# A two-block transformer kernel: the norm boundaries of block 2 multiply x by the root of the mean square, and a token's scale is applied when a product leaves PSUM

## The chip, the cores and the metric

The kernel runs on one core of a Trainium2 chip. The metric is the device time of one execution in microseconds (us), of which three runs are shown below; less is better. One further execution was profiled, and its trace is what the rows below come from.

## The reference

Everything is float32, for 256 tokens of width 1024. Block 1 (a recurrent mixer, a windowed attention and an FFN) is the same in both kernels except for its very last step. Block 2 takes the 256 tokens with 16 meta tokens ahead of them (272 columns) through two layers, and each layer crosses three norm boundaries:

```python
def rmsnorm(x, gain):
    xf = x.astype(jnp.float32)
    y = xf * lax.rsqrt(jnp.mean(xf * xf, axis=-1, keepdims=True) + RMS_EPS)
    return (y * gain.astype(jnp.float32)).astype(x.dtype)

def swiglu(h, w_gu, w_down):
    gate, up = jnp.split(h @ w_gu, 2, axis=-1)
    return (jax.nn.silu(gate) * up) @ w_down

for l in range(DEPTH_2):
    h = h + 0.5 * rmsnorm(swiglu(rmsnorm(h, g_pre_ffn1[l]), w_ffn1_gu[l], w_ffn1_down[l]), g_post_ffn1[l])
    mix = token_mixer(rmsnorm(h, g_pre_mix[l]), key_valid, ...)
    h = h + rmsnorm(mix, g_post_mix[l])
    h = h + 0.5 * rmsnorm(swiglu(rmsnorm(h, g_pre_ffn2[l]), w_ffn2_gu[l], w_ffn2_down[l]), g_post_ffn2[l])
```

The token mixer projects h by one wide matrix, runs softmax attention over 8 heads ("fox") and gated linear attention over 4 heads ("gla"), merges both under two sigmoid gates and projects again.

## The kernel before

Activations lie with features on the 128 partitions: x is 8 tiles of 128 x 272. A weight matrix streams through in panels. SyncE loads a panel into `land` (two slots, by the panel's parity), ScalarE rounds it to fp32r into `w_hi` (`split_hi`, L615), VectorE subtracts to get `w_lo` (`split_lo`, L622), and TensorE does three matmuls for each 128x128 tile: w_hi by h_hi, w_hi by h_lo, w_lo by h_hi (`tile_mm`, L640 to L642). While TensorE works on panel p, ScalarE and VectorE split panel p+1's successor of the same parity, always one panel ahead of need. `section` runs such a stage, two panels for each pass of a hardware loop, the last ones written out.

An FFN is 22 gate/up panels of 16 tiles (48 matmuls; `pe_project`, `act_gate_up`, `dve_gate_up`) and 8 down panels of 22 tiles (`pe_down`, `act_products`, `dve_products`). In a gate/up panel ScalarE takes the sigmoid of the gate from PSUM (L931), VectorE multiplies twice from PSUM (L945, L947), and both split the result into a_hi (L934) and a_lo (L953). PSUM has room for two gate/up panels.

At a boundary the last panel's squares close the sum `ssum`; `pe_stat` spreads their mean over the partitions with one matmul by `mean_ones` (L795, in full float32, two passes); ScalarE takes the root (`act_root`, L805), VectorE the reciprocal (L811), then for each of 8 tiles f = f * gain * rstd (L914) and x = x + f (L917). `act_pre_sums` squares x (L820), `pe_pre` sums the squares (L870), and a second root and a second reciprocal follow before `dve_pre_apply` normalises (L849), ScalarE rounds h_hi (L834), and VectorE subtracts h_lo (L860). Only then does the next section's first matmul start. Block 2 has six such boundaries, called b=1 to b=6 here: b=1 and b=4 lead from a down section into a gate/up section, b=2 and b=5 from a down section into the mixer's projection (whose first three panels have 8 tiles), b=3 and b=6 from the mixer's output projection (two output tiles to a panel) into a gate/up section.

In the mixer, 14 projection panels are cut in halves ("chunks", 24 matmuls each, `pe_chunk`), and TensorE places the small matmuls of fox and gla between them in an order written out by hand in `pe_mixer`. ScalarE empties most chunks from PSUM, taking the sigmoid at once where the chunk is a merge gate (L1781), VectorE the rest (L1798); a chunk's split is by `act_chunk_split` and `dve_chunk_split`, in the program order of those engines. GpSimd zeroes some tiles and copies fox's keys (L1936).

Of the kernel before, what the change touches and what calls it, by code (L numbers as in the profile page):

```python
# [922 lines left out]


# [1746 lines left out]
```

## Time and profile before

| | us |
|---|---|
| three runs | 2294.39, 2298.12, 2304.79 (median 2298.12) |
| the profiled execution | 2301.5 |
| its span in the trace | 2299.7 |
| TensorE matmul busy | 2038.5 (89%) |
| VectorE busy | 1357.4 (59%) |
| ScalarE busy | 953.1 (41%) |
| GpSimd busy | 115.8 (5%) |
| mean granted TensorE clock | 0.909 of full |

A matmul's record runs from its start to its modelled end, so records overlap, and the pace of a stretch is the distance between starts. Idle time in brackets names the instruction that ended it. A window of the rows below runs from the last matmul of a section to the end of the next one's first panel; its last numbers are the granted clock, the busy share of DMA and GB/s. The chain of waits follows the work that ended last back to the start.

### The profile page before, as it was taken

What the parts mean: (1) busy time and instruction counts of PE and PEld (TensorE: products, weight loads), DVE (VectorE), ACT (ScalarE), POOL (GpSimd) and SP (SyncE); (2) the same over time, 40 slices, a digit from 0 to 9 for tenths busy, and PEclk for the clock granted to TensorE, in tenths of its full rate; (3) what the DMA queues carried; (4) which work ended last, traced back from release to release, by engine and by line L of the source; (5) the groups of instructions that cost most, each with busy time, mean ns of one, the idle gap of its engine ahead of it and who ended that gap; (6) DMA issues with size and microseconds to landing.
All of it is one profiled execution on the core that took longest, in us unless ns stands there. A gap on an engine that the chain in (4) does not pass through costs nothing.

```text
span 2299.7 us, 38236 instructions
## 1 busy us (share of the span) xinstructions
PE 2038.5 (89%) x14904; PEld 1949.6 (85%) x14904; DVE 1357.4 (59%) x2065; ACT 953.1 (41%) x1382; POOL 115.8 (5%) x138
## 2 busy tenths in 40 slices
PE   8899548888789988998999879997999799798997
PEld 7899438886679988997888869997999788787997
DVE  5977545444676556555655575655655565566664
ACT  2333243332355434543443345533553354345542
POOL 0510001000000000000300000000000200000000
PEclk7899677777799999999999899998999999798998
DMA  7575000000335534552422244552455233253552
GB/s 316 201 259 218 0 24 1 0 0 18 113 128 182 198 131 146 172 198 97 147 74 94 83 156 146 166 193 99 164 181 185 97 101 106 76 166 126 183 199 94
DMA packets 43384, 301.21 MB, mean 131 GB/s; under 512 B 4689, under 2 KB 6881, under 8 KB 11025
## 3 DMA queue, kind: packets, MB, share of 16 engines
q1 hardware_dynamic: 42688, 296.90, 37.1%
q0 software_dynamic: 592, 2.87, 0.4%
q8 instruction: 74, 1.21, 0.2%
q14 instruction: 30, 0.24, 0.0%
HBM read 298.70 MB, written 1.05 MB: 130 GB/s over the span
## 4 chain that ended last, share of the span: by engine, by line
PE 78%; DVE 11%; ACT 4%; DVEq 3%; issue 2%; DMA 1%; POOL 0%; ACTq 0%; POOLq 0%; SPq 0%
PE acc L640 20%; PE acc L642 20%; PE acc L641 20%; DVE w_lo L622 3%; ACT w_hi L615 2%; PE acc L2012 1%; PE mb L870 1%; DVE rstd L811 1%; PE mb L709 1%; PE mb L1458 1%; PE acc L1458 1%; PE mb L1984 1%; PE acc L1455 1%; DVE f L914 1%; DVEq L1020 1%
## 5 line engine op out<-in xcount | busy, mean ns | idle before, releaser
L640 PE MATMUL acc<-h_hi,w_hi 128*128 128x272 f32 (+1 forms) x3040 | 893.5, 294 | 66.2 <-DVE w_lo L622 30.4
L642 PE MATMUL acc<-h_hi,w_lo 128*128 128x272 f32 (+1 forms) x3040 | 884.0, 291 | 0.0
L641 PE MATMUL acc<-h_lo,w_hi 128*128 128x272 f32 (+1 forms) x3040 | 882.9, 290 | 0.0
L622 DVE TENSOR_TENSOR w_lo<-land,w_hi 128x2048 fp32r<-128x2048 f32 (+2 forms) x257 | 590.7, 2300 | 230.0 <-ACT w_hi L615 229.3
L640 PEld LDWEIGHTS acc<-h_hi,w_hi 128*128 128x128 f32 x3040 | 590.9, 194 | 74.7 <-issue 38.5
L642 PEld LDWEIGHTS acc<-h_hi,w_lo 128*128 128x128 f32 x3040 | 590.7, 194 | 0.0
L641 PEld LDWEIGHTS acc<-h_lo,w_hi 128*128 128x128 f32 x3040 | 590.4, 194 | 0.2
L615 ACT ACTIVATE w_hi<-land 128x2048 fp32r<-128x2048 f32 (+2 forms) x257 | 490.8, 1911 | 224.7 <-PE acc L642 158.6
L640 PE MATMUL acc<-a_hi,w_hi 128*128 128x272 f32 (+1 forms) x880 | 251.0, 285 | 0.8 <-DVE w_lo L622 0.7
L642 PE MATMUL acc<-a_hi,w_lo 128*128 128x272 f32 (+1 forms) x880 | 250.5, 285 | 0.0
L641 PE MATMUL acc<-a_lo,w_hi 128*128 128x272 f32 (+1 forms) x880 | 250.0, 284 | 0.0
L931 ACT ACTIVATE sig<-acc 128x272 f32<-128x272 f32 (+1 forms) x110 | 43.3, 394 | 305.3 <-PE acc L642 305.3
L640 PEld LDWEIGHTS acc<-a_hi,w_hi 128*128 128x128 f32 x880 | 165.4, 188 | 1.8 <-DVE w_lo L622 1.8
L641 PEld LDWEIGHTS acc<-a_lo,w_hi 128*128 128x128 f32 x880 | 165.8, 188 | 0.0
L642 PEld LDWEIGHTS acc<-a_hi,w_lo 128*128 128x128 f32 x880 | 165.3, 188 | 0.0
L881 ACT ACTIVATE sq_post<-acc 128x256 f32<-128x256 f32 (+1 forms) x64 | 23.8, 391 | 263.8 <-PE acc L642 263.8
L945 DVE TENSOR_TENSOR t_ff<-sig,acc 128x272 f32<-128x272 f32 (+1 forms) x110 | 47.5, 432 | 131.6 <-ACT sig L931 131.6
L898 DVE COPY f<-acc 128x256 f32<-128x256 f32 (+3 forms) x64 | 27.7, 433 | 148.7 <-ACT sq_post L881 147.8
L870 PE MATMUL mb<-sq,mean_ones 128*128 128x272 f32 (+1 forms) x128 | 52.3, 570 | 41.3 <-ACT sq L820 40.8
L870 PEld LDWEIGHTS mb<-sq,mean_ones 128*128 128x128 f32 x128 | 28.4, 266 | 64.8 <-ACT sq L820 55.5
L640 PE MATMUL acc<-y_hi,w_hi 128*128 128x256 f32 (+1 forms) x192 | 57.4, 299 | 16.1 <-DVEq L506 13.6
L931 ACT ACT_TABLE_LOAD x50 | 64.2, 1283 | 0.9
(473 smaller groups left out, 2445.3 us busy)
## 6 DMA issues: line engine op xcount, KB each, us to landing
land<-in_w_gu SPq DMA_DIRECT2D x110, 1024.0 KB, 4.9
land<-in_w_in SPq DMA_DIRECT2D x65, 1024.0 KB, 4.9
land<-in_w_down SPq DMA_DIRECT2D x40, 1408.0 KB, 6.1
ada_first<-in_w_ada SPq DMA_DIRECT2D x24, 1024.0 KB, 8.4
land<-in_w_ab SPq DMA_DIRECT2D x24, 512.0 KB, 3.6
land<-in_w_out SPq DMA_DIRECT2D x12, 1024.0 KB, 4.9
land<-in_w_in_single SPq DMA_DIRECT2D x6, 512.0 KB, 3.5
const<-in_const POOLq DMA_DIRECT2D x1, 1134.0 KB, 5.3
```

The source lines that it names most:

```text
L615: k.nc.scalar.activation(k.w_hi[:, p.par, 0:size * P], k.land[:, p.par, 0:size * P], ACT.Copy).then_inc(k.hi_ready, 1)
L622: k.nc.vector.tensor_tensor(k.w_lo[:, p.par, 0:size * P], k.land[:, p.par, 0:size * P], k.w_hi[:, p.par, 0:size * P].bitcast(F32), ALU.sub ...
L640: mm(out, k.w_hi[:, par, c], hi, start=start, stop=False)
L641: mm(out, k.w_hi[:, par, c], lo, start=False, stop=False)
L642: return mm(out, k.w_lo[:, par, c], hi, start=False, stop=stop)
L709: last = k.nc.tensor.matmul(k.mb[:, 2, n * 2 + o:n * 2 + o + 1], w[:, o, t], k.csil_mean[:, t:t + 1], start=t == 0, stop=t == KT - 1)
L870: k.nc.tensor.matmul(k.mb[:, 3, 0:W.stop - W.start], k.mean_ones[:, :], k.sq[:, t % 2, W], start=t == 0, stop=t == KT - 1).then_inc(k.sq_u ...
L881: k.nc.scalar.activation(k.sq_post[:, 2 * p.par + o, W], k.acc[:, 2 * p.par + o, 0:n], ACT.Square).then_inc(k.sq_post_ready, 1)
L898: v.tensor_copy(f, k.acc[:, 2 * p.par + o, 0:n])
L931: k.nc.scalar.activation(k.sig[:, p.par, W], k.acc[:, 2 * p.par, 0:n], ACT.Sigmoid).then_inc(k.sig_ready, 1)
L945: v.tensor_tensor(k.t_ff[:, p.par, W], k.sig[:, p.par, W], k.acc[:, 2 * p.par, 0:n], ALU.mult)
L1458: last = mm(bank[:, 1, c * P + lo:c * P + hi], m["x_bd"][:, c, :], m["xr"][:, c, lo:hi], start=True, stop=True)
```

## The change

In words, with the root r = sqrt(mean f^2 + eps) of the branch's output f: the kernel before builds x' = x + gain * f / r and then normalises x'. The changed kernel builds z = x * r + gain * f, which is r times x', and does not normalise it: h_hi and h_lo are split from z * gain, the projection runs on that, and each column (token) of the product is multiplied by 1 / sqrt(mean z^2 + eps * r^2) as it leaves PSUM.

- At the end of a section (`act_products_z`, `dve_products_z`) the gain is applied as f leaves PSUM, ScalarE loads the table of the root early (`warm`), and the second panel of the next section is split into a third weight buffer, `w3_hi` and `w3_lo`. `pe_stat_z` adds the last panel's squares by matmul.
- `act_z`, `dve_z` make z, h_hi and h_lo. `pe_project_z` runs the next section's first panel tile by tile as h_lo comes, with nine float32 matmuls of z's squares (eight tiles and the eps term) among its own, and the second panel from the third buffer.
- `dve_scale` takes the reciprocal of the scale (into `ssum`'s place). Gate/up panels (`act_gate_up_z`, `dve_gate_up_z`) multiply gate and up by it first (`t_ff`, `g_ff`), then take the sigmoid from SBUF, and do a_lo a panel later. In the mixer every chunk leaves PSUM by a VectorE multiply, and ScalarE takes the gates' sigmoids from SBUF afterwards.
- After two gate/up panels (in the mixer, after the three small panels) `dve_undo` takes 1/r, and GpSimd restores x' = z / r with one instruction over all 8 tiles (`pool_z`). In the mixer GpSimd's zeroing comes after that.
- In the mixer, TensorE does one more chunk ahead of gla's output matmuls (and the rest of gla moves by one chunk), on VectorE and ScalarE likewise.

```diff
+def pe_project_z(k, pe, b, start, count, tiles, W, loop=0):
...
+    p = Panel.of(start, loop)
+    panel_begin(k, pe, p)
+    for t in range(KT):
+        pe.wait_ge(k.hl_ready, (b + 1) * KT + (t + 1))
+        for o in range(tiles):
+            last = tile_mm(k, k.acc[:, 2 * p.par + o, 0:n], p.par, o * KT + t, k.h_hi[:, t, W], k.h_lo[:, t, W],
+                           t == 0, t == KT - 1)
+        if t == KT - 1:
+            last.then_inc(k.panel_done, 1)
+        if t > 0:
+            square_sum(t - 1)
+    square_sum(KT - 1)
+    square_sum(KT)
```

```diff
+    for o in range(tiles):
+        pe.wait_ge(k.sq_post_ready, b * KT + KT - tiles + o + 1)
+        r = k.nc.tensor.matmul(stat, k.mean_ones[:, :], k.sq_post[:, 2 * last.par + o, W], start=False,
+                               stop=o == tiles - 1)
+    r.then_inc(k.stat_done, 1)
...
+    def one(t, p, ahead_size):
+        act.wait_ge(k.panel_done, p.count(3))
+        for o in range(tiles):
+            k.nc.scalar.activation(k.sq_post[:, 2 * p.par + o, W], k.acc[:, 2 * p.par + o, 0:n],
+                                   ACT.Square).then_inc(k.sq_post_ready, 1)
+        if ahead_size == "same":
+            split_hi(k, act, p.ahead2(), size)
+        elif ahead_size == "next":
+            split_hi(k, act, p.ahead2(), nxt)
+            split_hi_third(k, act, Panel.of(start + count + 1, loop), nxt)
+            k.nc.scalar.activation(k.warm[:, b:b + 1], k.eps[:, 0:1], ACT.Sqrt)
+    section(act, start, count, one, loop, ("next", None), unrolled=True)
...
+    def square(t):
+        act.wait_ge(k.sq_used, first + t + 1)
+        a(k.sq[:, (first + t) % 2, W], k.x[:, t, W], ACT.Square).then_inc(k.sq_ready, 1)
+    act.wait_ge(k.stat_done, b + 1)
+    act_root(k, post)
+    for t in range(KT):
+        act.wait_ge(k.z_ready, (b - 1) * KT + (t + 1))
+        a(k.h_hi[:, t, W], k.x[:, t, W], ACT.Copy, scale=gain(t)).then_inc(k.hh_ready, 1)
+        if t > 0:
+            square(t - 1)
+    square(KT - 1)
+    act.wait_ge(k.sq_used, first + KT + 1)
+    a(k.sq[:, (first + KT) % 2, W], k.root[:, W], ACT.Square, scale=float(np.sqrt(8 * EPS))).then_inc(k.sq_ready, 1)
+    act.wait_ge(k.sq_used, first + KT + 3)
+    a(k.scale[:, W], k.mb[:, 2, 0:W.stop - W.start], ACT.Sqrt).then_inc(k.scale_root, 1)
+
+
...
+    v = k.nc.vector
...
+    for t in own:
+        v.tensor_tensor(k.x[:, t, W], k.x[:, t, W], k.root[:, W], ALU.mult)
+    dve.drain()
...
+        v.tensor_tensor(k.x[:, t, W], k.x[:, t, W], k.f[:, t, W], ALU.add).then_inc(k.z_ready, 1)
...
+    def rest(t):
+        dve.wait_ge(k.hh_ready, (b + 1) * KT + (t + 1))
+        v.scalar_tensor_tensor(k.h_lo[:, t, W], k.x[:, t, W], gain(t), k.h_hi[:, t, W].bitcast(F32), ALU.mult,
+                               ALU.subtract).then_inc(k.hl_ready, 1)
+    for t in range(KT):
+        z(t)
+        if t > 1:
+            rest(t - 2)
+    rest(KT - 2)
+    rest(KT - 1)
...
+def dve_undo(k, dve, b, W):
+
+    k.nc.vector.reciprocal(k.rstd[:, W], k.root[:, W]).then_inc(k.r_ready, 1)
...
+    g.tensor_tensor(k.x[:, :, W], k.x[:, :, W], over(k.rstd[:, W], KT), ALU.mult)
+    pool.drain().then_inc(k.x_done, 1)
...
+    def one(t, p, ahead_size):
+        ahead(split_hi, k, act, p, ahead_size, GU_K)
+        act.wait_ge(k.t1_ready, z * FT + (t + 1))
+        k.nc.scalar.activation(k.sig[:, p.par, W], k.t_ff[:, p.par, W], ACT.Sigmoid).then_inc(k.sig_ready, 1)
+        act.wait_ge(k.a_ready, z * FT + (t + 1))
+        k.nc.scalar.activation(k.a_hi[:, bass.ds(t, 1), W].rearrange("p a n -> p (a n)"), k.a_ff[:, p.par, W],
+                               ACT.Copy).then_inc(k.ah_ready, 1)
...
+    def one(t, p, ahead_size, behind=True):
+        dve.wait_ge(k.panel_done, p.count(3))
+        v.tensor_tensor(k.t_ff[:, p.par, W], k.acc[:, 2 * p.par, 0:n], c, ALU.mult).then_inc(k.t1_ready, 1)
+        v.tensor_tensor(k.g_ff[:, p.par, W], k.acc[:, 2 * p.par + 1, 0:n], c, ALU.mult).then_inc(k.acc_free, 1)
+        if behind:
+            rest(t - 1, 1 - p.par)
+        ahead(split_lo, k, dve, p, ahead_size, GU_K)
+        dve.drain()
+        dve.wait_ge(k.sig_ready, i * FT + (t + 1))
+        v.tensor_tensor(k.t_ff[:, p.par, W], k.sig[:, p.par, W], k.t_ff[:, p.par, W], ALU.mult)
+        dve.drain()
+        v.tensor_tensor(k.a_ff[:, p.par, W], k.t_ff[:, p.par, W], k.g_ff[:, p.par, W],
+                        ALU.mult).then_inc(k.a_ready, 1)
+    one(0, Panel.of(start, loop), "same", False)
+    one(1, Panel.of(start + 1, loop), "same")
+    dve_undo(k, dve, b, W)
+    section(dve, start + 2, GU - 2, lambda t, p, s: one(t + 2, p, s), loop, nxt)
+    dve.drain()
+    rest(GU - 1, Panel.of(start + GU - 1, loop).par)
```

```diff
-        k.nc.vector.tensor_copy(dst(i), k.acc[:, 2 * p.par:2 * p.par + tiles, 0:n]).then_inc(k.acc_free, 1)
-        if signal is not None:
-            k.nc.vector.drain().then_inc(signal, 1)
+        k.nc.vector.tensor_tensor(dst(i), k.acc[:, 2 * p.par:2 * p.par + tiles, 0:n], over(k.scale[:, 0:n], tiles),
+                                  ALU.mult).then_inc(k.acc_free, 1)
         ahead(split_lo, k, dve, p, ahead_size, size)
     section(dve, start, count, one, loop, nxt)
...
+def act_chunk_gate(k, act, l, c):
+
+    r, o = divmod(c, 2)
+    if o == 0:
+        act.wait_ge(k.chunk_free, l * MIXED + r + 1)
+    else:
+        act.wait_ge(k.acc_free, mixed_panel(l, r).count(3))
+    return k.nc.scalar.activation(chunk_tile(k, l, c), chunk_tile(k, l, c), ACT.Sigmoid)
...
@@ -1917,7 +2198,8 @@
         pool.wait_ge(k.dec_mm, l)
     pool.dma_start(k.wal[:, :], flat(d["wal"], l)).then_inc(k.dec_in, 16)
     steps, first = fox_steps(l)
-    pool.wait_ge(k.hl_ready, (l * 3 + 4) * KT)
+    pool_z(k, pool, l * 3 + 2, W2)
+    pool.wait_ge(k.panel_done, Panel.of(M_LAYER + L_SINGLE + 1, l * (L_PANELS // 2)).count(3))
     g.memset(k.sel8[:, :, :].bitcast(F32), 0.0)
...
+    pe_chunk(k, pe, l, at + 6)
 
     for s in STREAMS:
...
             last = mm(gla_banks(k, "mean", s)[h][:, 0:TOK], k.mean_ones[:, :], k.g[s]["sq"][:, h, :], start=True,
                       stop=True)
...
     dve_chunk_evac(k, dve, l, at + 6)
+    dve_chunk_split(k, dve, l, at + 6)
+
...
             last = v.tensor_copy(k.g[s]["o"][:, h, :], gla_banks(k, "o", s)[h][:, 0:TOK])
         last.then_inc(k.gla_copied, 1)
-    dve_chunk_split(k, dve, l, at + 6)
-
-    for c in range(at + 7, at + 9):
-        s = c - (at + 7)
+    dve_chunk_split(k, dve, l, at + 7)
+
+    for c in range(at + 8, at + 10):
+        s = c - (at + 8)
         dve_chunk_evac(k, dve, l, c)
```

The three stretches below show what moved on VectorE. The first is b=1, from the last down panel of block 1's FFN to the next section. Before:

```order
L811 RECIPROCAL rstd<-root 128x256
L914 SCALAR_TENSOR_TENSOR f<-f,fold,rstd 128x256 x2
L917 TENSOR_TENSOR x<-x,f 128x256 x2
L914 SCALAR_TENSOR_TENSOR f<-f,fold,rstd 128x256 x2
L917 TENSOR_TENSOR x<-x,f 128x256 x2
L914 SCALAR_TENSOR_TENSOR f<-f,fold,rstd 128x256 x2
L917 TENSOR_TENSOR x<-x,f 128x256 x2
L914 SCALAR_TENSOR_TENSOR f<-f,fold,rstd 128x256 x2
L917 TENSOR_TENSOR x<-x,f 128x256 x2
L918 MEMSET ssum 128x272
L622 TENSOR_TENSOR w_lo<-land,w_hi 128x2048 x2
L811 RECIPROCAL rstd<-root 128x272
```

and now:

```order
L636 TENSOR_TENSOR w_lo<-land,w_hi 128x2048
L647 TENSOR_TENSOR w_lo<-land,w_hi 128x2048
L1042 TENSOR_SCALAR f<-acc,fold 128x256
L1092 TENSOR_TENSOR x<-x,root 128x272 x8
L1098 TENSOR_TENSOR x<-x,f 128x272 x3
L1102 SCALAR_TENSOR_TENSOR h_lo<-x,vec,h_hi 128x272
L1098 TENSOR_TENSOR x<-x,f 128x272
L1102 SCALAR_TENSOR_TENSOR h_lo<-x,vec,h_hi 128x272
```

The first reciprocal is gone, the two splits of 2048 stand ahead of the last panel's evacuation, and z's first parts follow eight multiplies.

The second is the start of the gate/up section behind b=1, after the last h_lo. Before, its first pass:

```order
L187 ISA
L945 TENSOR_TENSOR t_ff<-sig,acc 128x272
L947 TENSOR_TENSOR a_ff<-t_ff,acc 128x272
L621 ISA
L622 TENSOR_TENSOR w_lo<-land,w_hi 128x2048
L953 ISA
L953 TENSOR_TENSOR a_lo<-a_ff,a_hi 128x272
L944 REGISTER_ALU
L945 TENSOR_TENSOR t_ff<-sig,acc 128x272
L947 TENSOR_TENSOR a_ff<-t_ff,acc 128x272
```

and now its first two panels:

```order
L1164 TENSOR_TENSOR t_ff<-acc,ssum 128x272
L1165 TENSOR_TENSOR g_ff<-acc,ssum 128x272
L636 TENSOR_TENSOR w_lo<-land,w_hi 128x2048
L1171 TENSOR_TENSOR t_ff<-sig,t_ff 128x272
L1173 TENSOR_TENSOR a_ff<-t_ff,g_ff 128x272
L1164 TENSOR_TENSOR t_ff<-acc,ssum 128x272
L1165 TENSOR_TENSOR g_ff<-acc,ssum 128x272
L1158 TENSOR_TENSOR a_lo<-a_ff,a_hi 128x272
L636 TENSOR_TENSOR w_lo<-land,w_hi 128x2048
L1171 TENSOR_TENSOR t_ff<-sig,t_ff 128x272
L1173 TENSOR_TENSOR a_ff<-t_ff,g_ff 128x272
L1121 RECIPROCAL rstd<-root 128x272
```

Five elementwise instructions instead of three stand in a panel (`ssum` is the scale), with the split of the weights ahead of two of them and the reciprocal of the root after the second panel.

The third is linear attention in the first layer. `gr` is its output gate, `gla_o` its output, `p` a chunk's tile. Before:

```order
L2311 TENSOR_SCALAR gla_scaled_187<-gla_state_186,gst 64x128 x2
L2311 TENSOR_SCALAR gla_scaled_195<-gla_state_194,gst 64x128 x2
L2318 TENSOR_TENSOR gr__171<-gr__171,p_160 128x1088
L622 TENSOR_TENSOR w_lo<-land,w_hi 128x2048
L2325 COPY gla_o_183<-mb 128x272 x2
L2325 COPY gla_o_191<-mb 128x272 x2
L2334 RECIPROCAL gla_sq_184<-gla_sq_184 128x544
L2337 SCALAR_TENSOR_TENSOR gla_o_183<-gla_o_183,vec,gla_sq_184 128x272 x2
L2340 TENSOR_TENSOR gla_o_183<-gla_o_183,gr__171 128x544
L622 TENSOR_TENSOR w_lo<-land,w_hi 128x2048
L2334 RECIPROCAL gla_sq_192<-gla_sq_192 128x544
L2337 SCALAR_TENSOR_TENSOR gla_o_191<-gla_o_191,vec,gla_sq_192 128x272 x2
```

and now:

```order
L2593 TENSOR_SCALAR gla_scaled_191<-gla_state_190,gst 64x128 x2
L2593 TENSOR_SCALAR gla_scaled_199<-gla_state_198,gst 64x128 x2
L2077 TENSOR_TENSOR p_164<-acc,ssum 128x272
L2600 TENSOR_TENSOR gr__175<-gr__175,p_164 128x1088
L636 TENSOR_TENSOR w_lo<-land,w_hi 128x2048
L2077 TENSOR_TENSOR p_164<-acc,ssum 128x272 x2
L2610 COPY gla_o_187<-mb 128x272 x2
L2610 COPY gla_o_195<-mb 128x272 x2
L636 TENSOR_TENSOR w_lo<-land,w_hi 128x2048
L2077 TENSOR_TENSOR p_164<-acc,ssum 128x272
L2620 RECIPROCAL gla_sq_188<-gla_sq_188 128x544
L2623 SCALAR_TENSOR_TENSOR gla_o_187<-gla_o_187,vec,gla_sq_188 128x272 x2
```

A chunk's multiply stands ahead of `gr`, the split behind it is one that TensorE now needs before gla's output matmuls, and the splits come ahead of the two long reciprocals.

## Rows read from the trace of the kernel before

**Rows 1.** The page, the chain that ended last, its shares by engine

```profile
PE 78%; DVE 11%; ACT 4%; DVEq 3%; issue 2%; DMA 1%; POOL 0%; ACTq 0%; POOLq 0%; SPq 0%
```

**Rows 2.** Windows, b=1 to b=6 (length; busy PE, PEld, DVE, ACT, POOL; clock; DMA)

```profile
850.80:879.20 28.40, 16.60 (x69) 13.09 (x69) 21.74 (x39) 14.19 (x24) 0.00 (x0) 0.70 0.21 74
1072.60:1096.20 23.60, 12.98 (x45) 8.83 (x45) 18.81 (x38) 10.42 (x21) 0.63 (x1) 0.78 0.14 45
1359.20:1386.10 26.90, 14.89 (x69) 11.38 (x69) 20.68 (x40) 12.89 (x24) 0.00 (x0) 0.81 0.23 77
1579.50:1607.40 27.90, 15.21 (x68) 11.76 (x69) 22.14 (x39) 14.23 (x24) 0.00 (x0) 0.76 0.21 75
1800.80:1824.20 23.40, 12.82 (x45) 8.60 (x45) 18.81 (x38) 10.41 (x21) 0.65 (x1) 0.78 0.13 46
2074.60:2101.50 26.90, 15.62 (x70) 12.21 (x70) 19.87 (x40) 12.62 (x24) 0.00 (x0) 0.68 0.23 78
```

**Rows 3.** Timeline of b=4: start, length, engine, line, x count, idle before

```profile
1579.53 0.40 ACT L881 ACTIVATE sq_post<-acc 128x272 f32<-128x272 f32 x1 [7.88 <-PE acc L642]
1580.97 0.73 PE L795 MATMUL mb<-ssum,mean_ones 128*128 128x272 f32 x2 [1.48 <-DVEq L910]
1581.73 0.49 ACT L805 ACTIVATE root<-mb,eps 128x272 f32<-128x272 f32 x1 [0.50 <-PE mb L795]
1582.25 1.85 DVE L811 RECIPROCAL rstd<-root 128x272 f32<-128x272 f32 x1 [1.43 <-ACT root L805]
1584.18 0.91 DVE L914 SCALAR_TENSOR_TENSOR f<-f,vec,rstd 128x272 f32<-128x272 f32 x2
1585.17 0.79 DVE L917 TENSOR_TENSOR x<-x,f 128x272 f32<-128x272 f32 x2
1599.33 0.57 PE L640 MATMUL acc<-h_hi,w_hi 128*128 128x272 f32 x1 [6.73 <-DVE h_lo L860]
```

**Rows 4.** Timeline, PE: four full-precision sums by `mean_ones` in the first layer

```profile
1273.72 1.08 PE L2092 MATMUL acc<-gla_sq,mean_ones 128*128 128x272 f32 x4
1274.64 1.08 PE L2092 MATMUL mb<-gla_sq,mean_ones 128*128 128x272 f32 x4
```

**Rows 5.** Windows inside the first panel behind b=4

```profile
1597.50:1604.00 6.50, 4.67 (x23) 4.71 (x24) 6.20 (x17) 3.54 (x9) 0.00 (x0) 0.56 0.49 197
1604.00:1610.00 6.00, 6.00 (x50) 6.00 (x49) 1.63 (x4) 3.70 (x4) 0.00 (x0) 1.00 0.00 0
```

**Rows 6.** Timeline, block 1's projection: GpSimd and VectorE at once

```profile
88.94 1.19 POOL L1225 TENSOR_TENSOR p_in<-p_in,c 128x512 f32 x1 [0.15 <-issue]
88.99 3.28 DVE L622 TENSOR_TENSOR w_lo<-land,w_hi 128x2048 fp32r<-128x2048 f32 x1
```

**Rows 7.** Timeline, a gate/up panel, and the split for the down panels

```profile
994.50 1.91 ACT L615 ACTIVATE w_hi<-land 128x2048 fp32r<-128x2048 f32 x1
994.63 0.44 DVE L945 TENSOR_TENSOR t_ff<-sig,acc 128x272 f32<-128x272 f32 x1 [1.29 <-ACT sig L931]
996.44 2.29 DVE L622 TENSOR_TENSOR w_lo<-land,w_hi 128x2048 fp32r<-128x2048 f32 x1 [0.85 <-ACT w_hi L615]
998.96 0.44 DVE L953 TENSOR_TENSOR a_lo<-a_ff,a_hi 128x272 f32 x1 [0.23 <-issue]
1000.69 0.44 DVE L945 TENSOR_TENSOR t_ff<-sig,acc 128x272 f32<-128x272 f32 x1 [1.29 <-ACT sig L931]
1003.13 3.09 DVE L622 TENSOR_TENSOR w_lo<-land,w_hi 128x2816 fp32r<-128x2816 f32 x1 [1.50 <-ACT w_hi L615]
```

**Rows 8.** Timeline of linear attention in the first layer, and one window

```profile
1257.30 1.29 DVE L2318 TENSOR_TENSOR gr__171<-gr__171,p 128x1088 f32<-128x1088 f32 x1
1257.41 0.45 PE L2081 MATMUL mb<-gla_at,gla_vt 68*128 68x68 f32 x1 [4.75 <-DVE gla_scaled L2311]
1284.13 0.59 PE L640 MATMUL acc<-h_hi,w_hi 128*128 128x272 f32 x1 [5.39 <-DVE w_lo L622]
...
1255.00:1272.00 17.00, 14.59 (x68) 14.62 (x69) 7.18 (x13) 3.05 (x5) 0.00 (x0) 0.50 0.18 63
```

More of the change, by code:

```diff
@@ L921, in dve_post, with z_squares, pe_stat_z @@
     dve.drain()
+def z_squares(b):
+    return 2 * KT + (b - 1) * (KT + 1)
+def pe_stat_z(k, pe, b, start, tiles, W, loop=0):
+    stat = k.mb[:, 3, 0:W.stop - W.start]
+    last = Panel.of(start + KT // tiles - 1, loop)
+    pe.wait_ge(k.sums_ready, b + 1)
+    k.nc.tensor.matmul(stat, k.mean_ones[:, :], k.ssum[:, W], start=True, stop=False)
+    for o in range(tiles):
[3 more added lines that the diff above has]
+    r.then_inc(k.stat_done, 1)
@@ new lines, in act_products_z @@
+def act_products_z(k, act, b, start, tiles, W, size, nxt, loop=0):
+    n = W.stop - W.start
+    count = KT // tiles
+    def one(t, p, ahead_size):
+        act.wait_ge(k.panel_done, p.count(3))
+        for o in range(tiles):
+            k.nc.scalar.activation(k.sq_post[:, 2 * p.par + o, W], k.acc[:, 2 * p.par + o, 0:n],
[7 more added lines that the diff above has]
+    section(act, start, count, one, loop, ("next", None), unrolled=True)
@@ new lines, in dve_products_z, with one @@
+def dve_products_z(k, dve, b, start, tiles, W, size, gain, nxt, loop=0):
+    n = W.stop - W.start
+    count = KT // tiles
+    v = k.nc.vector
+    v.memset(k.ssum[:, :], 0.0)
+    dve.drain()
+    def one(idx, p, ahead_size):
+        dve.wait_ge(k.panel_done, p.count(3))
+        for o in range(tiles):
+            t = idx * tiles + o
+            dve.wait_ge(k.sq_post_ready, b * KT + (t + 1))
+            r = v.tensor_scalar(k.f[:, t, W], k.acc[:, 2 * p.par + o, 0:n], gain(t), None, ALU.mult)
+            if o == tiles - 1:
+                r.then_inc(k.acc_free, 1)
+            if idx < count - 1:
+                v.tensor_tensor(k.ssum[:, W], k.ssum[:, W], k.sq_post[:, 2 * p.par + o, W], ALU.add)
+            dve.drain()
+        if ahead_size == "same":
+            split_lo(k, dve, p.ahead2(), size)
+        elif ahead_size == "next":
+            v.drain().then_inc(k.sums_ready, 1)
+            split_lo(k, dve, p.ahead2(), nxt)
+            split_lo_third(k, dve, Panel.of(start + count + 1, loop), nxt)
+    section(dve, start, count, one, loop, ("next", None), unrolled=True)
@@ new lines, with act_z @@
+POOL_TILES = range(0)
+def act_z(k, act, b, post, W, gain):
+    a = k.nc.scalar.activation
+    first = z_squares(b)
+    def square(t):
[13 more added lines that the diff above has]
+    a(k.scale[:, W], k.mb[:, 2, 0:W.stop - W.start], ACT.Sqrt).then_inc(k.scale_root, 1)
@@ new lines, in act_gate_up_z @@
+def act_gate_up_z(k, act, i, start, W, nxt, loop=0):
+    z = i - 1
+    def one(t, p, ahead_size):
[5 more added lines that the diff above has]
+                               ACT.Copy).then_inc(k.ah_ready, 1)
+    section(act, start, GU, one, loop, nxt)
@@ L2352, in dve_mixer @@
     dve.drain()
+    dve.wait_ge(k.mix_gates, l + 1)
 def program_tensor(k, pe):
```

243 lines of the change are left out of this document (169 added, 74 removed).

## The prediction

> **What bounds the kernel now.** I read the head of the page first, then the chain that ended last, then windows over the six boundaries of block 2, then timelines inside one boundary, one gate/up panel and one linear attention. TensorE is 78% of the chain and VectorE 11% [rows 1]: the kernel is a TensorE stream with holes in which VectorE works alone. The largest of them are the boundaries. From the last matmul of a section to the end of the next section's first panel they take 28.4, 23.6, 26.9, 27.9, 23.4 and 26.9 us, 157.1 together [rows 2]. At b=4 the first matmul of the new section comes at 1599.33, 19.8 us after the last square began, and the rest of the window is the first panel itself [rows 3]. The reader is to see two things more. The chain at the boundary runs through two reciprocals of 1.85 each and pairs of elementwise instructions at 0.91 and 0.79 for two [rows 3]. And the clock is 0.56 of full behind the hole, then 1.00 [rows 5]: the first 4.7 us of the panel run at the lower level, 1.2 GHz, after TensorE had been nearly idle, which costs about 2.5 us.
>
> In a steady gate/up panel nothing waits but VectorE and ScalarE: a panel takes 1000.69 - 994.63 = 6.06 us, 48 matmuls at 0.126, and the idle time before L945 and before the split shows the spare time [rows 7].
>
> **The new boundary.** Times run from the end of the section before. Square of the last tile 0.43, the mean's matmuls to 1.2, root to 1.7 (both as in rows 3, with handovers). Then eight x*root on VectorE at the pitch of the pair L917, 0.37 each: 2.95, and 0.1 of drain, to 4.75. Three z adds (1.1) and the first h_lo (0.46, half of L914's pair), with ScalarE's h_hi beside them, to 6.4. So the first matmul comes after 6.4 us instead of 19.8.
>
> The first panel is now slower. It has its 48 matmuls (6.05) and nine float32 sums by `mean_ones`. Such a sum of the same size costs 0.46: two of them in 1274.64 - 1273.72 = 0.92 [rows 4]; nine make 4.1. VectorE's z and h_lo come at 0.83 a tile, TensorE needs 6 x 0.126 + 0.46 = 1.2, so TensorE sets this pace. The clock costs 2.5 as before (bounds: 0, since the hole is a third as long; 9, if the whole stretch stays at 1.2 GHz). That is 6.4 + 6.05 + 4.1 + 2.5 = 19.1 for b=1 and b=4. At b=3 a second square and a second matmul stand at the head: 20.1. At b=6 the same with 256 columns: 19.5. At b=2 and b=5 a panel has 8 tiles, VectorE sets the pace: 6.4 + 7 x 0.78 + 0.4 + three last sums 1.4 + clock 1.5 = 15.2. The sum is 2 x 19.1 + 20.1 + 19.5 + 2 x 15.2 = 108.2, against 157.1: **48.9 us saved**. The second panel's weights come from the third buffer, split before the boundary while TensorE works on the last down panels, where both engines are idle; I cost this at nothing, and without that cover it would be 2.3 a boundary.
>
> **What is given back in the gate/up sections.** First, x' is restored by one GpSimd instruction of 8 x 272 = 2176 elements a partition. The nearest row is GpSimd's two-input instruction of 512 elements, 1.19 us [rows 6], so 4.25 x 1.19 = 5.06. The VectorE split that ran with it took 3.28 instead of 2.29 [rows 6, 7]: it stood still for nearly all of GpSimd's 1.19. So I let VectorE's instructions with two SBUF operands stand still until GpSimd is done. With T the end of the first panel: VectorE evacuates panel 1 and splits for panel 3; panel 2 ends at T+6.05, its two multiplies, a_lo, the split (which waits for w_hi, 8.1 to 10.6) and two multiplies end at 11.6; reciprocal to 13.5; GpSimd runs from 13.5 to 18.55. VectorE gets through the next two multiplies, then a_lo and the split of the fifth panel wait, and that split is ready at 21.3. TensorE wants it after panels 2 to 4, at T+18.15. So it waits 3.2 us, in four sections: **-12.8** (bounds 0, if they do not block, and -18, if the multiplies from PSUM block too).
>
> On these multiplies the Trainium skill, "SBUF — State Buffer", section "Who interferes with whom", bears: a VectorE instruction with at most one SBUF input stays off the ports shared with GpSimd, one with two SBUF inputs does not while GpSimd reads. No row here shows the first half. By it the wait is the 3.2 above; by the opposite, the two multiplies (0.96) would come late too and the time would be 4 us longer. The trace agrees on the second half, by the 3.28 in rows 6, and this half is what speaks against the change.
>
> Second, the ends of the sections. In the last two gate/up panels the splits are of 2816 (VectorE 3.09 instead of 2.29, ScalarE about 0.6 longer too) [rows 7]. The new order has one cycle through both engines: w_hi to w_lo 1.94, w_lo to the next instruction 2.52, two multiplies 0.96, handover 0.1, a_hi with overlap 0.3, together 5.8 [rows 7]. Against 6.06 it fits, by 0.2. With the longer splits it is 7.2, and the last a_lo comes 9.05 after the last panel where the 22nd tile of the first down panel is due at 21 x 3 x 0.126 = 7.9. So -1.15 each, **-4.6**. Third, the section of 256 columns has panels of 5.68, 0.1 shorter than the cycle; it slips **-1.5** in its 22 panels.
>
> **The mixer.** All chunks leave PSUM by VectorE now, 0.44 each, in a part where TensorE is the bound and VectorE has idle time; I cost that at nothing. GpSimd's restore falls behind the three small panels, its zeroing comes later but before the keys are due (about 4 us of slack): nothing. If this slack were gone, each microsecond would count twice, once per layer. Linear attention: before, TensorE waits 4.75 for the scaled state and 5.39 later for a split behind a long reciprocal [rows 8]. Now the chunk ahead of the outputs waits for a split that stands behind the state's instructions, an evacuation 0.44, `gr` 1.29 and its own 2.29, to 1257.3 + 4.0 = 1261.3: a hole of 8.6 from 1252.7 instead of 4.75. In return the outputs find everything ready, and the splits now stand ahead of the reciprocals, so most of the 5.39 goes. I take 0 for each layer, between -3 (only the longer hole counts) and +4.
>
> **The sum.** 48.9 - 12.8 - 4.6 - 1.5 = 30.0. The profiled execution took 2301.5, its span 2299.7; it is 3.4 above the median 2298.1. So 2301.5 - 30.0 - 3.4 = **2268**.
>
> **The rivals.** (1) GpSimd's restore costs nothing: VectorE is idle enough or does not stand still. For it: the split in rows 6 still ran 3.28, not 3.28 + a whole extra; against: 0.99 of 1.19 is nearly all. The time is 2268 - 13 = 2255. (2) The clock. In the window of rows 8 TensorE is busy for 14.59 of 17.00 and has 0.50 all along, after small matmuls and holes. The interleaved first panels have float32 sums and waits between their matmuls, and so might stay at 1.2 GHz: 10.2 us of work become 19, 6.3 more than the 2.5 counted, in four boundaries, and 4.5 in two, 34 in all: 2302, no change. Against: 0.56 turned to 1.00 within 5 us in rows 5, with work as dense. A linear attention that loses 4 in both layers together with half of this lands in the same place, within 0.5%. (3) **Slower.** The cycle through ScalarE and VectorE in a gate/up panel is longer than TensorE's panel. It counts 88 times (22 panels in the sections behind b=1, 3, 4 and 6). From (30.0 / 88) = 0.34 over 6.06 it eats the whole gain; if each of four handovers costs 0.2 more than I took (0.23 stands before L953 in rows 7), the cycle is 6.65 and the loss 52: 2320. For it: only 0.2 of slack. Against: I took durations and handovers from the rows of the very panel. (4) That the earlier start is not reached, because z waits for GpSimd's restore of the boundary before: this has been done for 100 us and more by then, and I give it nothing.
>
> **The numbers.** Something under 0.5%, 11.5 us, can't be told from no change here. The forecast has 0.66, with its own range from 2250 to 2286 (linear attention and the clock's bounds, without their extremes); rival 1 has 0.13, rival 2 0.13, rival 3 0.08. Faster by over 0.5% (under 2286.6) are the forecast and rival 1: 0.79. Same: 0.13. Slower: 0.08. The range reaches from 2243, below rival 1 by a clock that costs nothing, to 2293, halfway into rival 2.
>
> **What would show it.** The first matmul 6 to 7 us after the last square at b=1, 2, 4, 5; windows of 19 and 15 us; a GpSimd instruction of about 5 us with an a_lo and a split beside it that end with it, and a hole of 3 us before the fifth panel; L1164 waiting for the panel, not ScalarE for VectorE, in steady panels. I am wrong if the clock in the first panels is 0.5 to their end, if holes come before every gate/up panel, or if TensorE waits in linear attention for over 12 us in sum.

## The result and the profile after

The changed kernel takes 2326.78 us (median of 4 runs, 2324.49 to 2328.81), the kernel before 2300.34 in the same comparison; the ratio is 1.0116, 95% interval 1.0088 to 1.0144. It is 26 us **slower**, where 2268 and faster was forecast, with a range up to 2293. The profiled execution took 2328.59, its span is 2326.8.

The chain by engine in the page after, which answers to [rows 1]: TensorE has fallen from 78% to 53% of it, VectorE has come up from 11% to 24% and ScalarE from 4% to 11%.

```profile
PE 53%; DVE 24%; ACT 11%; issue 5%; DVEq 4%; DMA 1%; ACTq 1%; POOL 0%; POOLq 0%; SPq 0%
```

The windows of the six boundaries after, which answer to [rows 2]: from the last matmul of a section to the start of the next one's second panel, so that the nine sums are inside.

```profile
852.80:871.60 18.80, 13.47 (x72) 11.52 (x70) 9.96 (x25) 7.93 (x19) 0.00 (x0) 0.82 0.20 78
1081.00:1097.10 16.10, 10.77 (x46) 8.35 (x46) 9.97 (x25) 7.93 (x19) 0.00 (x0) 0.79 0.03 13
1360.80:1380.10 19.30, 13.46 (x70) 11.81 (x71) 11.39 (x27) 8.33 (x21) 0.00 (x0) 0.82 0.27 98
1588.60:1608.10 19.50, 14.17 (x71) 12.09 (x70) 9.97 (x25) 7.96 (x19) 0.00 (x0) 0.82 0.15 64
1816.60:1831.90 15.30, 9.96 (x47) 7.62 (x46) 9.97 (x25) 7.94 (x19) 0.00 (x0) 0.89 0.05 21
2086.90:2105.90 19.00, 13.42 (x69) 11.95 (x70) 10.92 (x27) 8.02 (x21) 0.00 (x0) 0.73 0.24 95
```

They sum to 108.0 (108.2 forecast) against 157.1: the boundaries do what was expected, 49.1 us saved, each within 0.9 of its own forecast. So the loss, and what uses up these 49.1, lies between the boundaries. The windows of the sections between the boundaries, before and after (same columns: length, then busy time of TensorE, its weight loads, VectorE, ScalarE, GpSimd, then the clock; of sections of the same length one stands, the one behind b=1 for b=3 and b=4 before, the one behind b=3 for b=4 after). Before:

```profile
879.20:1072.60 193.40, 193.39 (x1536) 192.98 (x1534) 106.37 (x109) 86.67 (x89) 0.00 (x0) 1.00 0.48 166
1096.20:1359.20 263.00, 243.15 (x1721) 228.12 (x1719) 152.24 (x272) 110.51 (x209) 21.50 (x23) 0.94 0.34 113
...
1824.20:2074.60 250.40, 229.39 (x1672) 215.66 (x1671) 145.90 (x239) 106.22 (x184) 21.05 (x22) 0.94 0.35 118
2101.50:2283.50 182.00, 181.63 (x1536) 181.23 (x1534) 103.74 (x108) 85.02 (x88) 0.00 (x0) 1.00 0.49 168
```

After:

```profile
871.60:1081.00 209.40, 198.18 (x1539) 195.74 (x1538) 131.75 (x157) 106.66 (x104) 5.44 (x2) 0.99 0.46 158
1097.10:1360.80 263.70, 240.00 (x1724) 224.37 (x1722) 169.85 (x297) 112.16 (x206) 21.81 (x23) 0.95 0.34 113
1380.10:1588.60 208.50, 197.98 (x1539) 195.55 (x1538) 133.89 (x157) 108.50 (x104) 4.87 (x1) 0.99 0.47 160
...
1831.90:2086.90 255.00, 227.78 (x1676) 212.71 (x1674) 163.67 (x265) 108.09 (x182) 21.88 (x23) 0.95 0.35 117
2105.90:2310.60 204.70, 188.42 (x1538) 185.85 (x1536) 126.56 (x155) 102.56 (x100) 4.59 (x1) 0.98 0.43 149
```

The four sections of gate/up and down panels are longer by 16.0, 15.1, 15.1 and 22.7, together 68.9 (18.9 forecast); the two mixers by 0.7 and 4.6 (0 forecast). Block 1 ended 2.0 later in this profiled execution; over the profiles of all kernels here its end moves between 847.7 and 852.9. The sum is 2.0 - 49.1 + 68.9 + 5.3 = 27.1, the difference of the two spans. One caution for windows of two profiled executions: in a steady panel the matmuls start every 0.1261 us in that of the kernel before, and every 0.1253 in those of the changed kernel, of the moved loop and of the kernel before with a copy more (below). Over a section this is about 1.3 us, and why it differs is open.

What fills the gate/up sections is seen in TensorE's timeline. A hole is a stretch in which TensorE is idle; the brackets have its length and what ended it. The first line is the long hole before the fifth panel. Behind it, from 933 on, a hole of 0.8 to 0.9 like the second line's comes once in 13.16 us, before every second panel (1.4 in the section of 256 columns).

```profile
894.16 0.49 PE L665 MATMUL acc<-h_hi,w_hi 128*128 128x272 f32 x1 [3.81 <-DVE w_lo L636]
...
946.85 0.39 PE L665 MATMUL acc<-h_hi,w_hi 128*128 128x272 f32 x1 [0.87 <-DVE w_lo L636]
```

Behind the long hole the clock is lower, as a window there shows. Its 0.66 is a mean: the first matmuls are 0.23 apart, at the lower level (1.2 GHz), the later ones 0.126, at the upper.

```profile
894.00:899.00 5.00, 4.84 (x26) 4.84 (x27) 3.51 (x7) 2.55 (x3) 0.00 (x0) 0.66 0.63 211
```

And this is ScalarE's timeline in the same section:

```profile
895.62 1.90 ACT L629 ACTIVATE w_hi<-land 128x2048 fp32r<-128x2048 f32 x1
...
901.18 0.43 ACT L1144 ACTIVATE a_hi<-a_ff 128x272 f32 x1 [3.34 <-DVE a_ff L1173]
901.67 1.28 ACT L629 ACT_TABLE_LOAD   x1
902.96 1.92 ACT L629 ACTIVATE w_hi<-land 128x2048 fp32r<-128x2048 f32 x1
904.90 1.28 ACT L1142 ACT_TABLE_LOAD   x1
...
908.46 0.43 ACT L1144 ACTIVATE a_hi<-a_ff 128x272 f32 x1 [1.83 <-DVE a_ff L1173]
908.80 1.90 ACT L629 ACTIVATE w_hi<-land 128x2048 fp32r<-128x2048 f32 x1
```

A pass of ScalarE's hardware loop, two panels, now loads two activation tables, 1.28 each. The first stands between a_hi and w_hi, on the way round from ScalarE to VectorE and back. From 902.96 to the next w_hi at 908.80 the cycle is 5.84; the other half of a pass, with the load in it, has 7.3 (895.62 to 902.96). Together that is the 13.16 of a pass, where TensorE needs 2 x 6.06. The second load, before the sigmoid, lies beside VectorE's split. The kernel before also loads a table in each pass, but one, before the sigmoid, in time in which ScalarE waits for a panel, as its timeline shows:

```profile
899.89 1.28 ACT L931 ACT_TABLE_LOAD   x1
903.40 0.40 ACT L931 ACTIVATE sig<-acc 128x272 f32<-128x272 f32 x1 [2.23 <-PE acc L642]
```

### The profile page after: what moved, and what is told of

It reads as the page before. It is cut to its first block, busy times and chain, and to the rows that moved or that the text cites. A ratio compares the mean times of both kernels' runs of the same rounds, so it can differ in the third digit from the quotient of the medians.

```text
span 2326.8 us, 38331 instructions
## 1 busy us (share of the span) xinstructions
PE 2041.1 (88%) x14932; PEld 1952.6 (84%) x14932; DVE 1441.2 (62%) x2229; ACT 1015.1 (44%) x1421; POOL 134.0 (6%) x146
## 3 DMA queue, kind: packets, MB, share of 16 engines
q8 instruction: 74, 1.21, 0.2%
## 4 chain that ended last, share of the span: by engine, by line
PE 53%; DVE 24%; ACT 11%; issue 5%; DVEq 4%; DMA 1%; ACTq 1%; POOL 0%; POOLq 0%; SPq 0%
PE acc L665 12%; PE acc L667 12%; PE acc L666 12%; DVE w_lo L636 11%; ACT w_hi L629 9%; DVE t_ff L1171 2%; DVE a_ff L1173 2%; PE acc L2294 1%; PE mb L686 1%; PE mb L775 1%; PE mb L1735 1%; PE acc L1735 1%; DVE a_lo L1158 1%; DVEq L1297 1%; PE mb L2266 1%
## 5 line engine op out<-in xcount | busy, mean ns | idle before, releaser
L666 PE MATMUL acc<-h_lo,w_hi 128*128 128x272 f32 (+1 forms) x2960 | 862.4, 291 | 0.0
L667 PE MATMUL acc<-h_hi,w_lo 128*128 128x272 f32 (+1 forms) x2960 | 860.2, 291 | 0.0
L665 PEld LDWEIGHTS acc<-h_hi,w_hi 128*128 128x128 f32 x2960 | 576.7, 195 | 145.4 <-issue 85.1
L1144 ACT ACTIVATE a_hi<-a_ff 128x272 f32 (+3 forms) x88 | 37.7, 429 | 247.1 <-DVE a_ff L1173 247.1
L1131 POOL TENSOR_TENSOR x<-x,rstd 128x2176 f32<-128x2176 f32 (+1 forms) x6 | 28.9, 4825 | 1295.6 <-DVE rstd L1121 1295.6
L1018 ACT ACTIVATE sq_post<-acc 128x272 f32<-128x272 f32 (+1 forms) x48 | 18.0, 392 | 176.0 <-PE acc L667 176.0
L1042 DVE TENSOR_SCALAR f<-acc,vec 128x272 f32<-128x272 f32 (+1 forms) x40 | 19.9, 497 | 81.2 <-ACT sq_post L1018 80.5
L2077 DVE TENSOR_TENSOR p<-acc,ssum 128x272 f32<-128x272 f32 (+1 forms) x56 | 24.3, 433 | 60.7 <-PE acc L667 60.5
L1158 DVE TENSOR_TENSOR a_lo<-a_ff,a_hi 128x272 f32 (+3 forms) x88 | 55.5, 631 | 3.5 <-ACT a_hi L1144 2.0
L666 PE MATMUL acc<-y_lo,w_hi 128*128 128x256 f32 (+1 forms) x192 | 55.2, 288 | 0.0
```

The costliest lines, as they stand in the source:

```text
L665: mm(out, k.w_hi[:, par, c], hi, start=start, stop=False)
L666: mm(out, k.w_hi[:, par, c], lo, start=False, stop=False)
L1131: g.tensor_tensor(k.x[:, :, W], k.x[:, :, W], over(k.rstd[:, W], KT), ALU.mult)
L1144: k.nc.scalar.activation(k.a_hi[:, bass.ds(t, 1), W].rearrange("p a n -> p (a n)"), k.a_ff[:, p.par, W], ACT.Copy).then_inc(k.ah_ready, 1)
L1158: v.tensor_tensor(k.a_lo[:, a, W].rearrange("p a n -> p (a n)"), k.a_ff[:, par, W], k.a_hi[:, a, W].rearrange("p a n -> p (a n)").bitcast( ...
L2077: k.nc.vector.tensor_tensor(chunk_tile(k, l, c), k.acc[:, 2 + o, 0:W.stop - W.start], k.scale[:, W], ALU.mult).then_inc((k.chunk_free, k.a ...
```

## The experiments

Two things were open: whether this load, or the longer row of VectorE instructions, makes the holes before every second panel (theories A and B; C: any load counts), and what the 3.8 us hole before the fifth panel is (D: GpSimd's one instruction holds VectorE; E: its total time counts). Linear attention was a third (F, G). All medians are those of a comparison's runs, with runs of the kernel before in the same comparison.

**The loop boundary moved** (e1_rotate). ScalarE does the same in the same order, but the first split stands ahead of the loop, and a pass begins with the sigmoid. (The loop has nine passes instead of ten; four panels are written out behind it instead of two.)

```diff
-    def one(t, p, ahead_size):
-        ahead(split_hi, k, act, p, ahead_size, GU_K)
+    def one(t, p, nxt_p, ahead_size):
         act.wait_ge(k.t1_ready, z * FT + (t + 1))
...
-    section(act, start, GU, one, loop, nxt)
+        if nxt_p is not None:
+            ahead(split_hi, k, act, nxt_p, ahead_size, GU_K)
+    ahead(split_hi, k, act, Panel.of(start, loop), "same", GU_K)
+    pairs = (GU - 4) // 2
...
```

> Theory A (a table load at the head of ScalarE's loop pass, between a_hi and w_hi, in the cycle of ScalarE and VectorE): the same instructions in the same order with the loop boundary moved behind the split, so that a pass begins with the sigmoid, should bring a pair of 272-wide panels from 13.16 us back to 12.1 and a 256-wide pair from 13.13 to about 11.7; eight pairs a section, so 3 x 8 x 1.05 + 8 x 1.4 = about 36 us less: 2291. Theory B (the five VectorE instructions and their handovers alone make the cycle too long): the holes before every second panel stay, within 5 us of 2327.

Measured: 2284.76 (10 runs, 2279.69 to 2289.33), ratio to before 0.9942, interval 0.9922 to 0.9961. That is 42 us less than the changed kernel (36 expected), and 0.6% **faster than the kernel before**. ScalarE's timeline there:

```profile
910.86 1.92 ACT L629 ACTIVATE w_hi<-land 128x2048 fp32r<-128x2048 f32 x1
912.79 1.28 ACT L1141 ACT_TABLE_LOAD   x1
914.09 0.43 ACT L1141 ACTIVATE sig<-t_ff 128x272 f32<-128x272 f32 x1
...
916.87 1.92 ACT L629 ACTIVATE w_hi<-land 128x2048 fp32r<-128x2048 f32 x1
```

One load a pass, behind w_hi, and w_hi starts every 6.01. Between the fifth panel and the end of the gate/up section no hole is left. The windows of the same four sections:

```profile
869.05:1068.45 199.40, 195.06 (x1539) 194.53 (x1538) 131.28 (x157) 93.31 (x93) 5.43 (x2) 0.99 0.48 165
1367.40:1567.65 200.25, 195.92 (x1539) 195.39 (x1538) 133.52 (x157) 95.04 (x93) 4.86 (x1) 0.99 0.49 167
1586.15:1786.35 200.20, 195.78 (x1539) 195.26 (x1538) 131.21 (x157) 93.19 (x93) 5.47 (x2) 0.99 0.48 164
2076.55:2268.75 192.20, 186.03 (x1538) 185.19 (x1536) 126.22 (x155) 87.33 (x89) 4.59 (x1) 0.98 0.46 159
```

They are 10.0, 8.3, 8.3 and 12.5 shorter, 39.1 together. The hole before the first down panel (0.84 at b=1), which the expectation left out, went as well behind b=1, 3 and 4. Theory A stands, B falls: the five VectorE instructions and their handovers fit into a panel of 272 columns. In the section of 256 columns they just don't: a pass there takes 11.56, against 11.36 in the kernel before.

**A sigmoid ahead** (e2_sigfirst). A 128x1 sigmoid (`warm`, from `eps`) at the head of each pass of the changed kernel.

> Theory A: a 128x1 sigmoid at the head of a pass takes away the second table load of the pass (40 loads fewer, 51 us less of ScalarE's busy time) but leaves the one between a_hi and w_hi, and adds itself, 0.2: the pair of panels stays at 13.2 or becomes 13.4; 2327 to 2335. Rival C (what counts is ScalarE's load as a whole, both table loads): half of the gain of the moved loop, about 2309.

Measured: 2321.87 (4 runs, 2318.74 to 2330.5), ratio 1.0112, interval 1.0066 to 1.0157: not to be told from the changed kernel's 1.0116, and 5 us under the range expected by theory A. ScalarE's timeline has one load a pass, and it is the one that counts:

```profile
923.62 0.43 ACT L1146 ACTIVATE a_hi<-a_ff 128x272 f32 x1 [3.25 <-DVE a_ff L1175]
924.07 1.28 ACT L1141 ACT_TABLE_LOAD   x1
925.36 0.20 ACT L1141 ACTIVATE warm<-eps 128x1 f32<-128x1 f32 x1
925.47 1.90 ACT L629 ACTIVATE w_hi<-land 128x2048 fp32r<-128x2048 f32 x1
```

So half of these loads went and no gain of that size with them: rival C, 2309, falls. The pass stays at 937.21 - 924.07 = 13.14.

**Two loads where nothing waits** (e8_before_copy). The kernel before, with a 128x1 copy at the head of the pass.

> The kernel before, with a 128x1 copy at the head of ScalarE's gate/up pass, so that it too loads two tables in each pass (50 loads more, 64 us of ScalarE's time). Theory A (only a load in the cycle costs; here both fall into ScalarE's idle 3.5 us a panel): within 3 us of the kernel before. Rival C (two loads a pass cost by themselves): 20 to 50 us slower.

Measured: 2304.32 (10 runs, 2298.65 to 2309.92) beside 2301.1, ratio 1.0019, interval 1.0002 to 1.0037. The 50 loads more, 64 us of ScalarE's time, cost 3 us in the medians and 8.5 at the upper end of the interval; the profiled span, 2296.8, is even 2.9 shorter than that of before. ScalarE's timeline shows both loads in the time in which it waits for a panel, with 0.69 left over:

```profile
896.21 1.28 ACT L932 ACT_TABLE_LOAD   x1
...
897.71 1.28 ACT L934 ACT_TABLE_LOAD   x1
899.69 0.40 ACT L934 ACTIVATE sig<-acc 128x272 f32<-128x272 f32 x1 [0.69 <-PE acc L643]
```

The place decides, not the number.

**The restore in pieces** (e3_pieces, on the changed kernel).

```diff
-    g.tensor_tensor(k.x[:, :, W], k.x[:, :, W], over(k.rstd[:, W], KT), ALU.mult)
+    for t in range(KT):
+        g.tensor_tensor(k.x[:, t, W], k.x[:, t, W], k.rstd[:, W], ALU.mult)
```

> Theory D (GpSimd's one instruction holds VectorE's two-operand instructions for its whole length): with eight instructions of 272 elements, VectorE gets in between; a_lo no longer takes 4.78, the hole of 3.8 before the fifth panel and the lower clock behind it (1.6) shrink to 1 to 2: four sections by 3.5 to 4.5, 2309 to 2313. Rival E (GpSimd's total time counts, however it is cut): within 4 us of 2327.

Measured: 2310.7 (8 runs, 2305.8 to 2313.94), ratio 1.0054, interval 1.0032 to 1.0076: 16 us less. First the changed kernel's timeline, GpSimd and VectorE in the same microseconds:

```profile
886.67 4.86 POOL L1131 TENSOR_TENSOR x<-x,rstd 128x2176 f32<-128x2176 f32 x1 [297.40 <-DVE rstd L1121]
886.71 0.43 DVE L1165 TENSOR_TENSOR g_ff<-acc,ssum 128x272 f32<-128x272 f32 x1
887.05 4.78 DVE L1158 TENSOR_TENSOR a_lo<-a_ff,a_hi 128x272 f32 x1
891.75 2.28 DVE L636 TENSOR_TENSOR w_lo<-land,w_hi 128x2048 fp32r<-128x2048 f32 x1
```

a_lo, with both operands in SBUF, takes 4.78 instead of 0.44. L1165, which has one operand in PSUM, ran at its usual 0.43 with GpSimd already at work. The timeline of the version in pieces:

```profile
881.75 8.76 POOL L1132 TENSOR_TENSOR x<-x,rstd 128x272 f32<-128x272 f32 x8 [297.39 <-DVE rstd L1121]
882.13 0.69 DVE L1159 TENSOR_TENSOR a_lo<-a_ff,a_hi 128x272 f32 x1
884.00 2.35 DVE L636 TENSOR_TENSOR w_lo<-land,w_hi 128x2048 fp32r<-128x2048 f32 x1 [1.18 <-ACT w_hi L629]
```

GpSimd needs 8.76 instead of 4.86. A piece takes 0.78 in the median over the kernel, where an eighth of the uncut instruction is 0.61, so about 1.4 of the 3.9 more are the pieces' own length. Of the rest, 2.0 are one piece that waited for VectorE: it began at 884.16, beside VectorE's split, and took 2.82. Nobody waited for GpSimd. VectorE loses tenths in each of five instructions, about 1.6 in all. The hole before the fifth panel is 1.0 (1.7 in the section of 256 columns). Theory D stands, and E falls: GpSimd's total time grew while the kernel's shrank.

**Both together** (e5_rot_pieces).

> The moved loop boundary and GpSimd's restore in eight pieces together. If the two causes are independent, the gains add: 2327 - 42 - 16 = 2269, with no hole over 1.5 before the fifth panel of a gate/up section. If the pieces only moved a delay into a slack that the loaded pass did not have, the gain of the pieces is smaller here: 2275 to 2280.

Measured: 2263.4 (4 runs, 2259.24 to 2270.5), ratio 0.9848, interval 0.982 to 0.9877, the best of all: 1.5% faster than before. The gains add: the pieces gain 21 us here and 16 in the changed kernel, a difference within the intervals. Three of its windows, the first gate/up and down section and the two mixers:

```profile
866.80:1063.00 196.20, 194.62 (x1539) 193.87 (x1538) 129.52 (x157) 92.56 (x93) 9.31 (x9) 1.00 0.49 168
1079.10:1339.85 260.75, 238.21 (x1724) 222.49 (x1722) 166.90 (x297) 112.28 (x206) 27.44 (x30) 0.96 0.35 114
...
1785.60:2036.05 250.45, 225.37 (x1676) 210.70 (x1674) 160.84 (x265) 107.96 (x182) 27.50 (x30) 0.96 0.36 120
```

The mixers are 3.0 and 4.6 shorter than in the changed kernel, and no longer than before: what they had lost came back with the cut restore.

**The restore late** (e7_rot_late): the moved loop, the restore uncut, with its reciprocal at the start of the down section. **Late and in pieces** (e9_rot_late_pieces).

> The moved loop boundary, GpSimd's restore uncut, but it and the reciprocal ahead of it at the start of the down section in the four gate/up sections (in the mixer nothing changes). Theory D (the lock counts only where VectorE has no slack; a down panel of 8.3 us leaves over 4): the holes of 3.5 to 3.9 with the lower clock behind them go, 4 x 5.3 = 21 less than the moved loop alone, 2264. Rival H (the restore delays a split of the down section by as much): 2280 to 2285.

> Moved loop boundary, restore in eight pieces, and reciprocal and restore at the start of the down section. Theory D: the restore in one piece there cost a hole of 1.3 in the down section; pieces remove it, and the reciprocal no longer stands in a gate/up panel (0.76 of hole in the version with pieces in place): 3 to 5 us under the version with pieces alone, 2259. Rival: the end of the gate/up section has no slack either, and it is 2263 or more.

Measured: 2271.47 (4 runs, ratio 0.9883, interval 0.9862 to 0.9903) and 2264.88 (4 runs, ratio 0.987, interval 0.9826 to 0.9914). Moved to the down section, the uncut restore gains 13 of the 21 expected, and rival H, no gain, falls: the long hole is gone. But there it holds another instruction with two SBUF operands (L1046, 4.50 instead of 0.43), and a hole of 1.34 follows. L1042, with an operand in PSUM, again ran undisturbed beside GpSimd, which was at work from 1007.12 for 4.89.

```profile
1007.39 0.50 DVE L1042 TENSOR_SCALAR f<-acc,vec 128x272 f32<-128x272 f32 x1
1007.80 4.50 DVE L1046 TENSOR_TENSOR ssum<-ssum,sq_post 128x272 f32<-128x272 f32 x1
```

In pieces the place makes no difference that can be measured (2264.88 and 2263.4); the 3 to 5 us expected did not show.

**Linear attention** (e4_gla): in the changed kernel, the outputs back where they were (`at + 7` to `at + 6` and so on, on three engines; VectorE's splits behind the reciprocals again).

> Only linear attention's outputs are put back one chunk earlier. Theory F (moving them cost more than it gave, in the second layer above all, where the mixer took 4.7 us longer): the holes of 8.6 and 8.9 go back to about 5, those behind the reciprocals come back at about 5; net 0 to -5 us, 2322 to 2327. Rival G (the new order pays, and the mixer's +5.5 us come from the evacuations on VectorE): 2328 to 2334.

Measured: 2326.85 (4 runs, 2324.87 to 2327.62), ratio 1.0127, interval 1.0089 to 1.0164: no difference in the median. The windows of its two mixers:

```profile
1092.10:1360.25 268.15, 244.93 (x1724) 228.84 (x1722) 169.98 (x297) 112.39 (x206) 21.83 (x23) 0.94 0.34 111
1830.40:2086.60 256.20, 231.33 (x1676) 216.29 (x1674) 163.50 (x265) 108.18 (x182) 21.91 (x23) 0.95 0.35 117
```

They are 4.5 and 1.2 longer than in the changed kernel. The idle time is not the reason: by these windows TensorE is idle for 23.2 and 24.9 here, and for 23.7 and 27.2 in the changed kernel. The changed kernel has one long hole in each layer (8.57 and 8.88) with two of about 2 behind it, this one two holes of nearly 5 (4.80 and 4.61 in the first layer). What is longer is the time TensorE is busy with the same matmuls, by 4.9 and 3.6: in the 20 us behind the first hole the granted clock is 0.57 here (1252.1 to 1272.1) and 0.74 in the changed kernel (1257.1 to 1277.1). In this profile block 1 was 5 us shorter, which hid the difference in the span. By the windows the later outputs pay, theory G; by the medians it stays open.

**The gate's multiplication behind the split** (e10_rot_pieces_gr, on the best version): `gr` and the chunk's split change places on VectorE.

> Moved loop boundary, pieces, and in linear attention the split of a chunk ahead of the multiplication of the output gate (1.29 us) on VectorE. If the hole of 8.6 is made of the work ahead of that split, it becomes 7.3 in both layers: 2 to 3 us under the version with pieces alone, 2261. If another engine sets it (ScalarE's w_hi), nothing moves, 2263.

Measured: 2264.92 (4 runs), ratio 0.9856, interval 0.9811 to 0.99. The holes shrank as expected, from 8.58 to 7.38 and from 8.9 to 7.67, but the medians don't show a gain. 2.4 us are at the edge of what four runs can tell.

## Why the prediction was wrong, by its own steps

- **The new boundary** was right: 108.0 where 108.2 was forecast. The single windows are off by -0.8 to +0.9, which cancels. The first matmul came 6.4 us after the last square began (852.90 to 859.26 at b=1), and the first panel with its nine sums took as long as worked out: a tile with its sum every 1.21 at the upper clock (1.2 forecast).

```profile
852.90 0.38 ACT L1018 ACTIVATE sq_post<-acc 128x256 f32<-128x256 f32 x1 [1.20 <-PE acc L667]
...
859.26 0.57 PE L665 MATMUL acc<-h_hi,w_hi 128*128 128x272 f32 x1 [5.23 <-DVE h_lo L1102]
```

- **The cycle in a gate/up panel is the step that failed.** "Against 6.06 it fits, by 0.2" counted ScalarE's instructions without the loads of tables. The 5.8 was right (5.84 in the half without a load), and it is not what a pass costs: one load of 1.28 in the cycle makes 7.3 of it, and TensorE waits 0.8 to 1.4 before every second panel. Removing it gave 42 us by the medians and 39 in the windows, where 0 had been counted. It could have been seen: the prediction followed VectorE's order, while the diff has ScalarE's pass begin with the split, and the trace of before has a load at the head of each pass, with its price (1.28).
- **Rival 3**, the slower side, had the place right, the cycle through ScalarE and VectorE, and the number near (2320), but named handovers as the cause and was given 0.08. The handovers were as in the rows of before.
- **GpSimd's restore** had the right mechanism and too small a size. 5.06 forecast, 4.86 measured; the hole of 3.2 was 3.81, 3.80, 3.78 and 3.96. The term forgot that a hole is paid twice: behind it the clock was 0.66 from 894 to 899, and the next four panels took 25.85 (894.16 to 920.01, where the next hole begins) instead of 4 x 6.06 = 24.2. So a section loses about 5.4, not 3.2. The two mixers, costed at 0, lose by the restore too (3.0 and 4.6, by the version with both). The other bound, that the multiplies from PSUM stand still too, did not come true (0.43).
- **The ends of the sections** were 0.8 to 0.9 for a_lo instead of 1.15 (1.2 with 256 columns), plus about as much again for the split in the changed kernel; with the moved loop the second is left only with 256 columns (1.04).
- **The section of 256 columns** lost 22.7, mostly by the load: with the moved loop it is 10.2. That is still 3.4 to 4.2 more than the others, which lose 6.0 to 6.9, where 1.5 was counted. The slip itself, a cycle 0.1 longer than TensorE's panel, is there (11.56 a pass, 5.78 a panel, against 5.68); the longer hole (3.91) and the split at the end add to it.
- **The mixers** lost 0.7 and 4.6 instead of 0; linear attention alone was as forecast in its hole (8.6 forecast, 8.57 measured).
- **The clock** in the first panels, rival 2, did not stay at the lower level: it was 0.73 to 0.89 over the windows after, and these were as long as forecast.

With the load out of the cycle (2284.76) the kernel lies 17 us above the forecast: about 9 are the restore beyond its 12.8 (4 x 2.2), 5 the mixers, and the rest is not put down to a step. With the restore cut as well (2263.4) it lies 5 below.

## What to carry to other kernels

In every gate/up loop here the first ScalarE instruction of a pass brought a table load with it, even a copy. Loops of copies alone did not: block 1's loop that starts at L1526 in the kernel before (three passes) and its projection loops have no load in the trace. What decides it in a loop with a second function is open. Where two engines hand work round in a cycle that is nearly as long as TensorE's panel, start the pass at an instruction that has something to hide behind, and look for such loads on the engine whose order the change touches, not only on the busiest one. A long GpSimd instruction beside a VectorE with no slack is cut into pieces: it then takes longer, and costs less.
